# A mixture-of-experts decoder step on one core: weight loads in another order from pass 25, another early quarter, one undivided transfer, and a rearranged tail

## The reference, cut to what matters

```python
def expert_block(args):
    tok, e = args
    h = xn[tok] @ w_gu[e] + b_gu[e]
    gate = jnp.minimum(h[:, :D_FF], SWIGLU_LIMIT)
    up = jnp.clip(h[:, D_FF:], -SWIGLU_LIMIT, SWIGLU_LIMIT)
    return ((up + 1.0) * gate * jax.nn.sigmoid(SWIGLU_ALPHA * gate)) @ w_down[e] + b_down[e]
```

## Time and profile before

| what | value |
|---|---|
| runs | 1285.73, 1285.91, 1288.38 us; median 1285.91 |
| profiled execution | 1287.98 us, span 1286.0 us, granted clock 0.996 |
| TensorE matmul busy | 1224.4 us (95%) |
| VectorE, ScalarE, GpSimd busy | 381.1, 192.5, 16.1 us |
| DMA moved | 463.72 MB, mean 361 GB/s |
| of it `w_gu` | 127 transfers of 2 MB and 2 of 1 MB |
| of it `w_down` | 32 of 2 MB, 32 of 1.5 MB, 32 of 0.5 MB |

### The profile page before, as it was taken

The page is one execution under the profiler, slowest core; times in us unless marked ns, Lnnn a source line. Parts: engine busy times, 40 slices in busy tenths (PEclk is TensorE's granted clock), DMA queues, the critical chain, the costliest instruction groups (busy, mean ns, idle before and its releaser), DMA issues.

```text
span 1286.0 us, 16610 instructions
## 1 busy us (share of the span) xinstructions
PE 1224.4 (95%) x6416; PEld 556.3 (43%) x6416; DVE 381.1 (30%) x921; ACT 192.5 (15%) x432; POOL 16.1 (1%) x28
## 2 busy tenths in 40 slices
PE   7999999999999999989899999999999998998998
PEld 3556778685533443323233333333433333332333
DVE  2555755324541222212121121222222121121223
ACT  3123234202301001100100001110010100000010
POOL 0000000011000000000000000000000000000000
PEclk9999999999999999999999999999999999999999
DMA  9787552598689999999999999999999999999991
GB/s 332 185 252 223 208 189 63 150 339 320 243 364 428 425 426 429 425 430 426 429 426 427 427 427 427 425 398 424 429 426 429 426 430 425 428 428 427 427 426 59
DMA packets 82306, 463.72 MB, mean 361 GB/s; under 512 B 20418, under 2 KB 35538, under 8 KB 57298
## 3 DMA queue, kind: packets, MB, share of 16 engines
q1 hardware_dynamic: 77650, 462.02, 89.1%
q10 hardware_dynamic: 4608, 1.05, 0.5%
HBM read 460.05 MB, written 5.09 MB: 362 GB/s over the span
## 4 chain that ended last, share of the span: by engine, by line
PE 61%; DMA 36%; DVE 1%; ACT 1%; issue 1%; SPq 0%; DVEq 0%
DMA arena<-w_gu 35%; PE banks L1238 19%; PE banks L1315 8%; PE banks L2174 6%; PE banks L626 4%; PE banks L806 2%; PE banks L1491 2%; PE banks L1210 2%; PE banks L1171 2%; PE banks L570 2%; PE banks L1269 1%; PE banks L2193 1%; PE banks L682 1%; PE banks L1192 1%; PE banks L695 1%; PE banks L1274 1%
## 5 line engine op out<-in xcount | busy, mean ns | idle before, releaser
L1238 PE MATMUL banks<-arena 128*64 128x512 f32 x1984 | 443.8, 596 | 35.1 <-DMA arena<-w_gu 34.7
L1238 PEld LDWEIGHTS banks<-arena 128*64 128x64 f32 x1984 | 136.1, 137 | 316.0 <-issue 242.7
L1315 PE MATMUL banks<-arena 128*64 128x512 f32 x1024 | 226.8, 595 | 0.0
L1412 DVE TENSOR_SCALAR arena<-banks 128x512 f32<-128x512 f32 x32 | 22.1, 691 | 405.6 <-PE banks L1238 383.5
L1315 PEld LDWEIGHTS banks<-arena 128*64 128x64 f32 x1024 | 73.6, 137 | 134.9 <-issue 129.7
L1370 ACT ACTIVATE arena<-arena 128x512 f32<-128x512 f32 x32 | 20.2, 630 | 548.5 <-DVE arena L1412 548.5
L2174 PE MATMUL banks<-arena 128*128 128x512 f32 (+1 forms) x192 | 79.1, 570 | 0.0
L1453 DVE TENSOR_TENSOR arena<-banks,arena 128x528 f32<-128x528 f32 x64 | 45.3, 708 | 94.1 <-PE banks L1210 94.1
L1171 PE MATMUL banks<-arena 128*64 128x512 f32 x256 | 61.3, 599 | 0.9 <-DVE arena L1405 0.9
L1210 PE MATMUL banks<-arena 128*128 128x264 f32 x256 | 61.2, 392 | 0.0
L626 PE MATMUL banks<-arena 128*128 128x264 f32 x256 | 60.0, 388 | 0.5 <-ACT arena L846 0.5
(11 more groups left out here) (366 smaller groups left out, 925.8 us busy)
## 6 DMA issues: line engine op xcount, KB each, us to landing
arena<-w_gu SPq DMA_DIRECT2D x127, 2048.0 KB, 23.4
arena<-w_down SPq DMA_DIRECT2D x32, 2048.0 KB, 24.5
arena<-w_down SPq DMA_DIRECT2D x32, 1536.0 KB, 22.5
arena<-w_in SPq DMA_DIRECT2D x8, 2048.0 KB, 13.2
arena<-w_down SPq DMA_DIRECT2D x32, 512.0 KB, 23.9
arena<-cache_moba_k SPq DMA_DIRECT2D x16, 256.0 KB, 2.8
arena<-cache_moba_v SPq DMA_DIRECT2D x16, 256.0 KB, 3.2
arena<-w_out SPq DMA_DIRECT2D x2, 2048.0 KB, 13.6
```

The lines of the kernel that those rows point to most:

```text
L1238: mm = nc.tensor.matmul(banks[64 * x:64 * x + 64, BG + b, :], xgT[:, c % 4, 64 * (c // 4):64 * (c // 4) + 64], w[:, D * b + 512 * x:D * b ...
L1315: mm = nc.tensor.matmul(banks[64 * x:64 * x + 64, BY, :], product[:, c, 64 * part:64 * part + 64], w[:, 512 * x:512 * x + 512], start=Fals ...
```

## The change

- **Order of the loads.** SyncE's last loop ends at pass 23 (`TURN` is 12). From then on the gates of pass q + 1 are asked for ahead of the down weights of pass q, up to pass 31; the down weights of 31 then come ahead of the gates of 32, and the down weights of 32 are last.
- **Another early part.** Of expert 1 the quarter 3 comes early, and the quarters 0 to 2 go straight into the slots that expert 0 leaves. The quarters of expert 2 are asked for one quarter sooner. Clearing `acc` waits for the end of pass 1's gates.
- **Undivided odd slot.** The first half of an odd place's down weights is one transfer of 2 MB; the other stays 1.5 + 0.5 MB. The router's small tensors move.
- **Pauses at the end.** Between the turns of pass 31 and its down product TensorE gets `gate_bias` of pass 32 (moved there) and one product into an unused bank; in the tail two tiles of sums are turned ahead of `turn_product`, with another such product.
- **Last sums.** The order is tile 0, 1 (first half), 0 (second half), the two 8-row sums side by side in one bank, 1 (second half). The second 8-row half lies on partitions 32 to 39. There are six stores.

```diff
-            src = t["w_gu"][1].rearrange("(s p c) n -> s p c n", p=P, c=2)[0]
+            src = t["w_gu"][1].rearrange("(s p c) n -> s p c n", p=P, c=2)[3]
...
-        odd_main = [at(k_at, 3, D), at(d_at + KC * TOK, 3, D)]
-        odd_rest = [at(m_at + 3 * D + 3 * D // 2, D), at(m_at + 2 * D, D)]
+        odd_first, odd_second, odd_last = at(k_at, 4, D), at(d_at + KC * TOK, 3, D), at(m_at + 2 * D, D)
...
-            if parity:
-                eng.dma_start(odd_main[part], src[:, 0:3, :]).then_inc(ring_in[RING + part], 16)
-                eng.dma_start(odd_rest[part], src[:, 3, :]).then_inc(ring_in[RING + part], 16)
+            if parity and part == 0:
+                eng.dma_start(odd_first, src).then_inc(ring_in[RING], 16)
+            elif parity:
+                eng.dma_start(odd_second, src[:, 0:3, :]).then_inc(ring_in[RING + 1], 16)
+                eng.dma_start(odd_last, src[:, 3, :]).then_inc(ring_in[RING + 1], 16)
...
-            pool.wait_ge(S["used"], 4)
+            pool.wait_ge(S["gu"], 2)
             nc.gpsimd.memset(acc, 0.0).then_inc(S["added"], 1)
...
-        LAST_TILES, LAST_BANKS = (0, 2, 1), (0, 1, 2, 3, 4, 6)
-        y_store_count = 16 * 5
+        LAST_SUMS = ((0, 0, 0), (1, 0, 1), (0, 1, 2), (2, 0, 3), (2, 1, 3), (1, 1, 4))
+        y_store_count = 16 * 6
...
-            for n in range(2):
-                pe.wait_ge(S["ykept"], 2 * passes - 1 + n)
-                for k, i in enumerate(LAST_TILES):
-                    r = ROWS[i]
-                    nc.tensor.matmul(banks[0:r, LAST_BANKS[3 * n + k], :], selT[:, P * i:P * i + r], y[:, 512 * n:512 * n + 512],
-                                     start=True, stop=True).then_inc(t_scat, 1)
+            for i, n, bank in LAST_SUMS:
+                if i == 0:
+                    pe.wait_ge(S["ykept"], 2 * passes - 1 + n)
+                if i < 2:
+                    nc.tensor.matmul(banks[:, bank, :], selT[:, P * i:P * i + P], y[:, 512 * n:512 * n + 512], start=True, stop=True).then_inc(t_scat, 1)
+                elif n == 0:
+                    for x in range(2):
+                        mm = nc.tensor.matmul(banks[32 * x:32 * x + DB, bank, :], selT[:, SEQ:TOK], y[:, 512 * x:512 * x + 512],
+                                              start=True, stop=True, tile_position=(0, 32 * x))
+                    mm.then_inc(t_scat, 1)
...
+        def keep_warm(n, bank):
+            for _ in range(n):
+                nc.tensor.matmul(banks[:, bank, :], ident, cst[:, 0:512], start=True, stop=True)
...
         def experts_sp(sp):
-            for s in range(1, 4):
-                sp.wait_ge(S["used"], s)
-                load_expert_slot(sp, 1, s)
+            for s in range(3):
+                sp.wait_ge(S["used"], s + 1)
+                load_expert_slot(sp, 1, s, turning=False)
...
             for s in range(1, 4):
-                if s < 3:
-                    sp.wait_ge(S["used"], 4 + s)
-                else:
-                    sp.wait_ge(S["gu"], 2)
+                sp.wait_ge(S["used"], 3 + s)
                 load_expert_slot(sp, e, s)
...
-            with sp.Fori(TWICE // 2 + 1, PAIRS) as k:
+            with sp.Fori(TWICE // 2 + 1, TURN) as k:
                 for q, parity in ((2 * k, 0), (2 * k + 1, 1)):
                     e = placed_expert(sp, q + 1)
                     load_gate_up(sp, e, q + 1)
                     load_down(sp, e, q, parity)
+            load_gate_up(sp, sp.value_load(order_i[0:1, 2 * TURN + 1:2 * TURN + 2], min_val=0, max_val=NEXP - 1), 2 * TURN + 1)
+            with sp.Fori(TURN, PAIRS - 1) as k:
+                for q, parity in ((2 * k + 1, 0), (2 * k + 2, 1)):
+                    load_gate_up(sp, placed_expert(sp, q + 1), q + 1)
+                    load_down(sp, placed_expert(sp, q), q - 1, parity)
+            load_down(sp, sp.value_load(order_i[0:1, LAST - 1:LAST], min_val=0, max_val=NEXP - 1), LAST - 2, 0)
+            last = sp.value_load(order_i[0:1, LAST:LAST + 1], min_val=0, max_val=NEXP - 1)
+            load_gate_up(sp, last, LAST)
+            load_down(sp, last, LAST - 1, 1)
...
+            gate_bias(pe, LAST, 0)
+            keep_warm(1, 7)
             down(pe, LAST - 1, 0, NEXP // 2 - 1, 1)
-            gate_up(pe, LAST, NEXP - 1, 0, None, last_pair)
+            gate_up(pe, LAST, NEXP - 1, 0, None, last_pair, biased=True)
             pe.wait_ge(S["added"], 4 * PAIRS + 1)
             for i in range(NT):
                 r = ROWS[i]
-                if i == 1:
+                if i == 2:
+                    keep_warm(1, 5)
                     turn_product(pe, LAST)
```

More of the change, by code:

```diff
@@ L415, in down_piece @@
         def down_piece(part, parity, nth):
+            if parity and part == 0:
+                return lambda c: odd_first[:, c, :], ring_in[RING], 16 * nth + 16
             if parity:
-                return lambda c: odd_main[part][:, c, :] if c < 3 else odd_rest[part], ring_in[RING + part], 32 * nth + 32
+                return lambda c: odd_second[:, c, :] if c < 3 else odd_last, ring_in[RING + 1], 32 * nth + 32
             s = expert_slot(4 + part)
@@ L1228, in gate_up @@
                 part = c // 2
-                s, value = piece_at(part, place)
-                first = isinstance(q, int) and q == 1 and part == 0
-                if c % 2 == 0 and first:
+                second = isinstance(q, int) and q == 1
+                s, value = (expert_slot(part), 32 + dense_count[expert_slot(part)]) if second else piece_at(part, place)
+                ahead = second and part == 3
+                if c % 2 == 0 and ahead:
                     pe.wait_ge(early_in, 32)
@@ L1234, in gate_up @@
                     pe.wait_ge(ring_in[s], value)
-                w = early[c] if first else ring[:, s, :].rearrange("p (c n) -> p c n", c=2)[:, c % 2, :]
+                w = early[c % 2] if ahead else ring[:, s, :].rearrange("p (c n) -> p c n", c=2)[:, c % 2, :]
                 for b in range(2):
@@ L1395, in keep_out @@
             if items is not None:
-                act.wait_ge(t_scat, 6 * items)
+                act.wait_ge(t_scat, 5 * items)
             for x in range(2):
@@ L1443, in select_by_slot @@
             else:
-                dve.wait_ge(t_scat, 6 * items)
+                dve.wait_ge(t_scat, 5 * items)
             nc.vector.tensor_scalar(selT, banks[:, BT, 0:TOK], slot_number, None, ALU.is_equal).then_inc(S["stkept"], 1)
@@ L1453, in add, with sum_rows, add_tokens @@
                 nc.vector.tensor_tensor(v, scatter_banks(c)[:, :, 0:TOK], v, ALU.add).then_inc(S["added"], 1)
[L1455 to L1462, removed]
+        def sum_rows(i, n):
+            return slice(32 * n, 32 * n + DB) if i == 2 else slice(0, P)
+        def add_tokens(dve, scattered):
+            for (i, n, bank), done in zip(LAST_SUMS, (1, 2, 3, 4, 4, 5)):
+                dve.wait_ge(t_scat, scattered + done)
+                rows = sum_rows(i, n)
+                v = sums_to[rows, i, 512 * n:512 * n + 512]
+                nc.vector.tensor_tensor(v, banks[rows, bank, :], v, ALU.add).then_inc(t_added, 1)
         def store_tokens(sp, before):
             y_prompt, y_sample = t["y_prompt"], t["y_sample"].rearrange("a b d -> (a b) d")
-            for count, i, cols in ((1, 0, slice(0, 512)), (3, 1, slice(0, 512)), (4, 0, slice(512, D)), (5, 2, slice(0, D)), (6, 1, slice(512, D))):
-                sp.wait_ge(t_added, before + count)
-                dst = y_sample if i == 2 else y_prompt[0, P * i:P * i + P, cols]
-                sp.dma_start(dst, sums_to[0:ROWS[i], i, cols]).then_inc(stored["y"], 16)
+            for count, (i, n, bank) in enumerate(LAST_SUMS):
+                cols = slice(512 * n, 512 * n + 512)
+                sp.wait_ge(t_added, before + count + 1)
+                dst = y_sample[:, cols] if i == 2 else y_prompt[0, P * i:P * i + P, cols]
+                sp.dma_start(dst, sums_to[sum_rows(i, n), i, cols]).then_inc(stored["y"], 16)
         def listed(eng):
@@ L1536, in ranks @@
                 return mm
-            def keep_warm(n):
-                for _ in range(n):
-                    nc.tensor.matmul(banks[:, 6, :], ident, cst[:, 0:512], start=True, stop=True)
             pe.wait_ge(r_chosen, 2)
@@ L1546, in route_pe @@
             gather_first(pe, 0, 1)
-            keep_warm(1)
+            keep_warm(1, 6)
             pe.wait_ge(r_chosen, 3)
@@ L2040, in experts_dve @@
                     cols = slice(512 * half, 512 * half + 512)
-                    nc.vector.tensor_tensor(sums_to[0:r, i, cols], banks[0:r, (BS, BX, BS)[i] + half, :], h[0:r, i, cols], ALU.add).then_inc(f_added, 1)
+                    nc.vector.tensor_tensor(sums_to[sum_rows(i, half), i, cols], banks[0:r, (BS, BX, BS)[i] + half, :], h[0:r, i, cols], ALU.add).then_inc(f_added, 1)
             select_by_slot(dve, PAIRS, slot_of[:, PAIRS:PAIRS + 1])
```

7 lines of the change are left out of this document (4 added, 3 removed).

## The result

The changed kernel takes 1273.3 us (median of 4 runs, 1272.4 to 1275.11); the kernel before took 1285.82 beside it (4 runs, 1285.29 to 1288.38). The ratio is 0.9903, with a 95% interval of 0.989 to 0.9917: 12.5 us less. The profiled execution took 1273.92 us, its span is 1272.0 us and its granted clock 1.000.

A forecast was written before the change was run, and what follows sets the result against it. The weight stream sets the time until pass 31, then TensorE sets the end. Terms 10.1 + 1.4 + 1.1 + 1.2 + 1.0 = 14.8 us, taken off the median 1285.91, give 1271.1 us; range 1268.8 to 1275, the forecast's own 1269 to 1273.

The forecast's parts named there:

- the new hole: Weight stream after the router: a hole of 2.1 us opens near 385 because the down pair isn't requested before 385.18.
- The order of the loads: Loads from pass 25: gates of pass 32 end at 1251.55 instead of 1261.65, 10.1 us saved, including down 31's slow stretch.
- The early part: Expert 1's early quarter: the hole at 369 to 375 shrinks by 3.5 us, a new one costs 2.1; gain 1.4 us.
- the 350 that the prediction named as a sign: Weight stream: over 350 GB/s in 369 to 375 would show the forecast right.
- The undivided half: Odd places' down weights: joining one divided half saves 0.095 us, for 12 places 1.1 us.
- The fillers: Tail: work in the pause lets the spread start 5.6 us after the gates' end and run at full clock, 1.2 us saved.
- The side-by-side sums: Last scatter: the two 8-row sums run side by side, so one sum of 1.0 us goes.
- A: Rival: the clock falls in the new order's waits, giving 1272.4 to 1274.5 us; chance 0.18.
- B: Rival: the early part and the undivided half bring nothing, giving 1273.6 us; chance 0.09.
- C: Rival: the reordering brings little, TensorE runs late or the last down pair binds; 1276 to 1281 us; chance 0.06.
- D: Rival: slower, half clock throughout from pass 25, 1301 us with a fall at some seven waits a pair; chance 0.04.
- The choice of pass 25: Start of the new load order: no gap in the stream, cost 0, covered by 25 us of queued work.

The follow-up runs named there:

- order_only: The kernel before with only SyncE's new order of loads from pass 25: 1276.49 us, ratio 0.9938 to the kernel before.
- before_again: The kernel before, unchanged, run once more for a second profile: 1284.65 us.
- pair_second: The changed kernel with the two side-by-side 8-row sums second instead of fourth: 1272.55 us, ratio 0.9902 to the kernel before.
- gates32_first: The changed kernel with the gates of pass 32 loaded ahead of the down weights of pass 31: 1292.35 us, ratio 1.0055 to the kernel before.
- turn14: The changed kernel with the gates ahead of the down weights from pass 29 instead of 25: 1276.78 us, ratio 0.9928 to the kernel before.

## Why the prediction was right, point by point

The forecast was 1271.1 us, the measured median 1273.3; the range of 1268.8 to 1275 held it, the forecast's own of 1269 to 1273 just missed it. The mechanism was right in each step that the traces show: the stream sets the end of gates 32 again, the new hole opened, the undivided half saved what it should. The sizes were too large for the order, the early part and the tail, and in part it is luck that the time came out so near.

**The order of the loads.** The last quarter lands at 1245.78 (forecast 1247.9 less 2.5 from the other parts, 1245.4) and TensorE waits 0.82 us for it. That this fits so well is partly luck: the 1247.9 came from an execution that had lost 1.3 us to the half clock near 794, which the changed kernel's profile doesn't have, and the other parts brought only 1.1 of their 2.5 us there (see the account). The term was 10.1 us, and it holds 1.6 us for the half clock of down 31. In order_only against before_again, two executions without that stretch, gates 32 end 906.4 and 914.9 us after the first gates: **8.5 us**. The prediction said so itself: "It includes the slow stretch of down 31". I took from one profiled execution, one of the longest of this kernel (1287.98 us, where the medians are 1285.4 to 1286.1), stretches of half clock that most executions have in other places or not at all, and then took the sum off the median. Against that execution's own time the sum gave 1273.2, and the profiled execution after took 1273.92; there the 1.3 us near 794, which the sum doesn't have, made up for nearly all that the early part and the undivided halves fell short of.

**The early part.** Forecast 1.4, measured 1.0 us in the traces up to pass 15, 0.7 at pass 31, and 1.2 in the runs. The new hole opened where it was expected; both holes are a little longer than the restart of 1.8 us made them, and 369 to 375 runs at 336 GB/s, just under the 350 that the prediction named as a sign.

**The undivided half.** Forecast 0.095 us each, measured 0.09 (29.47 instead of 29.56), so the 1.1 us for twelve stand.

**The tail.** The fillers were to give 1.2 us. From the end of gates 32 to the start of down 32 the changed kernel needs 5.7 us, before_again 5.8 and the profile before 7.2: at full clock the fillers give 0.1 there, and 1.5 only where the clock would have fallen. In proportion this term was the furthest off. The side-by-side sums were to give 1.0: six sums in 5.99 us became five in 4.84. But VectorE adds 8 rows as slowly as 128 (0.68 us), so the last add ends 5.95 us after the scatter began instead of 6.71, 0.8 us less. Behind the last add 2.9 us pass to the end of the span instead of 2.45, in all versions with six stores and the old place of the pair; pair_second has 2.75. Why was not taken apart.

**The account.** From the first gates to the end of the span before_again takes 937.9 us (344.87 to 1282.8) and the changed kernel's profile 927.8 (344.18 to 1272.0), neither with half clock under TensorE's work: **10.1 us less**, where the sum had 14.8. It is 8.5 for the order, 1.1 for the early part and the undivided halves together (gates 32 end 906.4 us after the first gates in order_only, 905.3 in the changed kernel), and 0.1 + 0.8 - 0.45 for the tail.

Alone, the early part and the undivided halves brought 0.7 and 1.1 us at pass 31. The landings in the traces show where the rest stays. Each transfer lands in 16 parts, and TensorE waits for the last of them. For the last quarter of pass 32 the mean of the 16 landings is 901.4 us after the first gates in order_only and 899.5 in the changed kernel, 1.9 us sooner; the last of the 16 is at 902.8 and 901.6, only 1.2 sooner. They are spread over 3.0 us instead of 2.4. Why they drift apart is open.

The measured 12.5 us are 2.4 more than these 10.1. Some 0.6 lie ahead of the first gates, which begin anywhere from 343.3 to 344.9 us in the profiles, with the change or without it; before_again has its half clock there. The median of the kernel before lies 1.2 us above before_again, and that of the changed kernel 0.6 under its profile. Part of this may be half clock, which the kernel before has more of (its mean granted clock over the 47 executions is 0.9979, the changed kernel's over four is 0.9988): two of the three places where the first profile lost it now have fillers, and one of these two stands ahead of a wait. That share was not measured by itself. The gains of the four parts alone (8.0, 1.2, 1.5 and 1.8 us) also add up to 12.5, but each is uncertain by 1 to 2 us.

**The rivals.** The time doesn't tell the forecast from A (1272.4 to 1274.5) or B (1273.6); the traces do, as far as one execution goes. A did not come in the profile: the waits for data from pass 25 on are at most 1.25 us, and no clock below 1.00 stands beside them. The other three executions have granted clocks of 0.997 and 0.999, and where they lost them isn't known. No short wait for data brought the clock down here; the one long wait, 17.5 us in gates32_first, did stand beside half clock. B fell by the holes and the periods. C was excluded here, but turn14 is its picture: TensorE late by what it could not work off. D never came near.

**What I had wrong without paying for it.** The choice of pass 25 looked free in my reasoning. It isn't: earlier, the stream runs dry; later, the lead can't be used.

## What to carry to other kernels

Read the end of a data-bound kernel backwards: not when the last byte lands, but which load lands last ahead of how much work; requests ordered by use shorten that work, though no byte moves sooner in all. Such an order needs time to pay: find the pass where the engine has caught up and count the spare time from there to the end. And before a term from one profiled execution goes into a sum against a median, ask whether it is in every execution; stretches of half clock are the first to doubt.

## What the runs showed of the hardware

Equal pauses of 1.75 to 1.88 us at the same place were followed by 3.4 us of half clock in one execution and by full clock in another of the same kernel. In a wait of 17.5 us the clock was at half for most of it (0.56 for 1224 to 1241), while some 40 waits of up to 1.25 us for weights left it at 1.00. A transfer of 2 MB in the full queue landed in 16 parts over 1.8 to 3.4 us (last gate quarter of pass 32, 14 profiles), and the work that needed it began with the last. Dividing a 2 MB transfer into 1.5 and 0.5 MB cost 0.09 us in this queue. A VectorE add of 8 x 512 elements from the sums takes 0.68 us, as long as one of 128 x 512.
